# Both orders of real and imaginary part from TensorE's transposes in a fused retention, state-space and FFN block

## The reference

```python
h = rmsnorm(x, norm_mix_g)
proj = h @ w_in                      # 2048 -> 5120: q, k, v, g, u of 1024 each
y_ret = retention_group(rope(q), rope(k), v, g, ret_gn_g)
y_ssm = s5_group(u, ...)             # 64 groups of 16 channels, 64 complex states each
x = x + concat([y_ret, y_ssm]) @ w_out
h = rmsnorm(x, norm_ffn_g)
x = x + (silu(h @ w_gate) * (h @ w_up)) @ w_down     # 2048 -> 5632 -> 2048
return rmsnorm(x, norm_final_g)
```

## Time and profile before

| | |
|---|---|
| median of 3 runs | 1171.8 us (1170.96 to 1172.73) |
| the profiled execution | 1172.48 us, of which the span of its records is 1170.7 us |
| PE busy | 1139.4 us, 97% of the span, 5632 matmuls |
| PE weight loads busy | 933.6 us, 80% |
| DVE busy | 714.3 us, 61% |
| ACT busy | 528.9 us, 45% |
| POOL busy | 91.8 us, 8% |
| mean granted TensorE clock | 0.987 |
| DMA | 226.37 MB, mean 193 GB/s |

### The profile page before, as it was taken

One profiled execution on the slowest core, in us unless ns is written; L12 is line 12 of the kernel. 1 busy time (PEld: TensorE's weight loads), 2 busy tenths in 40 slices (PEclk: granted clock), 3 DMA queues, 4 the chain that ended last, 5 costly groups with the idle time before them and its releaser, 6 DMA issues.

```text
span 1170.7 us, 15157 instructions
## 1 busy us (share of the span) xinstructions
PE 1139.4 (97%) x5632; PEld 933.6 (80%) x5632; DVE 714.3 (61%) x776; ACT 528.9 (45%) x617; POOL 91.8 (8%) x132
## 2 busy tenths in 40 slices
PE   8999969999999999999999999999999999999996
PEld 6777747788988888888888888888888888888885
DVE  7998787744774664555564645555464645555465
ACT  6756424344663554433434343443434343343443
POOL 8120231330100000000000000000000000000001
PEclk9998988999999999999999999999999999999998
DMA  9783676676565567656566666656566666656652
GB/s 360 263 228 105 195 203 197 192 212 197 186 206 179 184 180 219 195 181 196 181 195 183 193 183 193 196 181 196 180 195 181 193 184 193 188 187 190 187 186 90
DMA packets 115416, 226.37 MB, mean 193 GB/s; under 512 B 8625, under 2 KB 13105, under 8 KB 114737
## 3 DMA queue, kind: packets, MB, share of 16 engines
q1 hardware_dynamic: 110816, 214.80, 59.6%
q0 software_dynamic: 4128, 10.36, 3.4%
q10 hardware_dynamic: 432, 0.67, 0.2%
HBM read 218.59 MB, written 5.11 MB: 191 GB/s over the span
## 4 chain that ended last, share of the span: by engine, by line
PE 89%; DVE 4%; DMA 3%; issue 1%; ACT 1%; POOL 0%; SPq 0%; POOLq 0%; ACTq 0%
PE ps L1329 28%; PE ps L1331 27%; PE ps L1330 27%; DMA raw<-in_w_in 2%; DVE w_lo L743 1%; DMA swapped<-state 1%; PE ps L1551 1%; PE ps L1624 1%; PE ps L1626 1%; PE ps L1625 1%; PE ps L1466 1%; PE ps L1384 1%; PE ps L1449 1%; PE ps L1484 0%; PE ps L1424 0%
## 5 line engine op out<-in xcount | busy, mean ns | idle before, releaser
L743 DVE TENSOR_TENSOR w_lo<-raw,w_hi 128x1024 fp32r<-128x1024 f32 x384 | 468.3, 1224 | 412.0 <-ACT w_hi L412 411.7
L412 ACT ACTIVATE w_hi<-raw 128x1024 fp32r<-128x1024 f32 x384 | 407.0, 1060 | 593.7 <-PE ps L1331 549.3
L1329 PE MATMUL ps<-w_hi,actA_hi 128*128 128x512 f32 x576 | 229.9, 399 | 8.0 <-DVE w_lo L743 8.0
L1331 PE MATMUL ps<-w_hi,actA_lo 128*128 128x512 f32 x576 | 225.9, 392 | 0.0
L1330 PE MATMUL ps<-w_lo,actA_hi 128*128 128x512 f32 x576 | 225.5, 392 | 0.0
L1329 PE MATMUL ps<-w_hi,h2B_hi 128*128 128x512 f32 x352 | 139.0, 395 | 0.0
L1331 PE MATMUL ps<-w_hi,h2B_lo 128*128 128x512 f32 x352 | 138.8, 394 | 0.0
L1330 PE MATMUL ps<-w_lo,h2B_hi 128*128 128x512 f32 x352 | 138.8, 394 | 0.0
L1329 PEld LDWEIGHTS ps<-w_hi,actA_hi 128*128 128x128 f32 x576 | 109.0, 189 | 33.6 <-DVE w_lo L743 7.4
L1331 PEld LDWEIGHTS ps<-w_hi,actA_lo 128*128 128x128 f32 x576 | 108.8, 189 | 23.4
L1330 PEld LDWEIGHTS ps<-w_lo,actA_hi 128*128 128x128 f32 x576 | 109.0, 189 | 21.4
(11 more groups left out here) (239 smaller groups left out, 987.1 us busy)
## 6 DMA issues: line engine op xcount, KB each, us to landing
raw<-in_w_gate SPq DMA_DIRECT2D x88, 512.0 KB, 3.7
raw<-in_w_up SPq DMA_DIRECT2D x88, 512.0 KB, 3.7
raw<-in_w_down SPq DMA_DIRECT2D x88, 512.0 KB, 3.8
raw<-in_w_in SPq DMA_DIRECT2D x80, 512.0 KB, 4.9
raw<-in_w_out SPq DMA_DIRECT2D x32, 512.0 KB, 4.6
k_tab<-k_scratch POOLq DMA_DIRECT2D x64, 64.0 KB, 3.6
raw<-in_ssm_w_glu SPq DMA_DIRECT2D x8, 512.0 KB, 3.5
xT<-in_xT SPq DMA_DIRECT2D x8, 256.0 KB, 6.2
```

The lines of the kernel that those rows point to most:

```text
L412: nc.scalar.activation(w_hi[:, s % SPL], raw[:, s % RAW], ACT.Copy).then_inc(S["high_done"], 1)
L743: tt(w_lo[:, s % SPL], raw[:, s % RAW], w_hi[:, s % SPL].bitcast(F32), ALU.subtract).then_inc(S["low_done"], 1)
L1329: mm(o, x_hi, h, start=first, stop=False)
L1331: return mm(o, x_lo, h, start=False, stop=last)
```

## The change

- `inputs_back(b)` makes four transposes instead of two: of `vt` columns 0 to 127 and of columns 64 to 191. `vt` is 64 columns wider, and ACT fills it with two copies, the second one repeating the first 64 columns behind the rest. The results stand in bank 6 instead of half of bank 7, and ACT copies them to `state` and to `swapped`, so `v_free` counts two per batch.
- The first exchange by DMA goes; `scan_states(h)` waits for `v_free` 8 or 16 instead. The exchange between scan and turn-back stays. POOL also sets the first column of `swapped` to zero. The second exchange of POOL's queue comes right behind `load_k(0)`.
- The four ACT steps of a phase table are done in four chunks, one in each (26 to 29, 31 to 34).
- `cl` has a fourth slot in the room of `wbT`; `CL_SLOT` and `CL_PRIOR` say which table uses which slot, and which `y_batch` frees it. The decay loads, which share the room, wait for `y_mm` 3.
- K tables 0 and 1 go to banks 4 and 5. K0 waits for all of `wbT`, K2 and later ones for `v_free` 16.
- New places for turn steps, decays, scans, turn-back, `cl`, K, Y and the first two heads.

```diff
@@ -79,6 +79,8 @@
 CBUF, TBUF = 3, 2
+CL_SLOT = (0, 1, 3, 2, 0, 1, 2, 0)
+CL_PRIOR = (None, None, None, None, 0, 1, 3, 4)
 PARAM_AT = 9
...
@@ -86,21 +88,22 @@
 ANGLE_AT = (23, 27)
-TURN_AT = (26, 30)
-DECAYS_AT = (28, 38)
+TURN_AT = (26, 31)
+DECAYS_AT = (30, 36)
 FACTOR_AT = 29
-SCAN_AT = (33, 42)
-BACK_AT = (37, 45)
-CL_AT = (29, 31, 34, 44, 47, 50, 56, 60)
-K_AT = (31, 34, 37, 46, 49, 52, 58, 62)
-Y_AT = (42, 45, 47, 54, 57, 60, 66, 70)
-Y_BANK = (7, 7, 7, 7, 7, 7, 6, 6)
+SCAN_AT = (32, 40)
+BACK_AT = (35, 45)
+CL_AT = (30, 36, 38, 42, 47, 50, 55, 60)
+K_AT = (33, 38, 40, 44, 49, 52, 57, 62)
+Y_AT = (43, 47, 49, 53, 57, 65, 67, 71)
+K_BANK = (4, 5, 6, 6, 6, 6, 6, 6)
+Y_BANK = (7, 7, 7, 7, 7, 6, 6, 6)
 QK_AT = tuple(GRP * (gi + 1) + 3 for gi in (4, 5, 6, 7))
...
 DECAY_LOAD = (55, 55, 65, 66, 70, 71, 80, 81)
-HEAD_AT = (62, 63, 65, 66, 75, 76, 78, 79)
+HEAD_AT = (61, 62, 65, 66, 75, 76, 78, 79)
 STATS_AT = (67, 71, 81, 83)
...
@@ -203,9 +206,11 @@
             [("wbT", [P, 2, BG, P], F32)],
+            [("cl_extra", [P, BG, LOC + 1, CH], F32)],
             [("dec", [P, 2, TOK, SEQ], F32), ("sT", [P, 2, TOK, SEQ], F32)],
...
         wbT, dec, sT = (m[k] for k in ("wbT", "dec", "sT"))
+        cl_slots = [cl[:, i] for i in range(CBUF)] + [m["cl_extra"][:]]
         cl_t = sb("cl_t", [P, BG, LOC + 1, CH])
...
@@ -215,7 +220,7 @@
         dtmp = sb("dtmp", [P, GROUPS // 4, CH])
-        m = overlay([("rope", [P, TOK, 2, HEAD_DIM], F32)], [("vt", [P, 2, P], F32)])
+        m = overlay([("rope", [P, TOK, 2, HEAD_DIM], F32)], [("vt", [P, 2, P + STATE], F32)])
         rope, vt = m["rope"], m["vt"]
...
@@ -242,7 +247,6 @@
         d_b, d_c = sem("d_b"), sem("d_c")
-        d_swap = [sem(f"d_swap{i}") for i in range(2)]
         d_swap_back = [sem(f"d_swap_back{i}") for i in range(2)]
...
@@ -332,7 +336,7 @@
-                    sp.wait_ge(S["v_mm"], NB)
+                    sp.wait_ge(S["y_mm"], 3)
                 else:
...
@@ -432,20 +436,23 @@
-            def turn_tables(h):
-
-
-                act.wait_ge(S["angles_ready"], h + 1)
+            def turn_table(h, step):
+
+
                 c, s = flat(cos[h][:]), flat(sin[h][:])
-                nc.scalar.activation(s, c, ACT.Sin, scale=vec[:, V_TURN:V_TURN + 1]).then_inc(S["turn_step"], 1)
-                act.wait_ge(S["turn_step"], 4 * h + 1)
-                nc.scalar.activation(c, c, ACT.Sin, scale=3.1415925).then_inc(S["turn_step"], 1)
-                act.wait_ge(S["turn_step"], 4 * h + 2)
-                nc.scalar.activation(c, c, ACT.Square, scale=float(np.sqrt(2.0))).then_inc(S["turn_step"], 1)
-                act.wait_ge(S["turn_step"], 4 * h + 3)
-                if h == 0:
-                    act.wait_ge(S["const_ready"], 1)
-                nc.scalar.activation(c, c, ACT.Identity, bias=ones[:], scale=-1.0).then_inc(S["turn_step"], 1)
+                if step == 0:
+                    act.wait_ge(S["angles_ready"], h + 1)
+                    ins = nc.scalar.activation(s, c, ACT.Sin, scale=vec[:, V_TURN:V_TURN + 1])
+                else:
+                    act.wait_ge(S["turn_step"], 4 * h + step)
+                    if step == 1:
+                        ins = nc.scalar.activation(c, c, ACT.Sin, scale=3.1415925)
+                    elif step == 2:
+                        ins = nc.scalar.activation(c, c, ACT.Square, scale=float(np.sqrt(2.0)))
+                    else:
+                        act.wait_ge(S["const_ready"], 1)
+                        ins = nc.scalar.activation(c, c, ACT.Identity, bias=ones[:], scale=-1.0)
+                ins.then_inc(S["turn_step"], 1)
...
@@ -533,16 +540,18 @@
                             act.wait_ge(S["zero_ready"], 1)
-                        nc.scalar.activation(state[:, s5_group(b), 1:],
-                                             ps[:, 7, 2 * P:4 * P].rearrange("p (g k) -> p g k", g=BG)[:, :, 0:NCH - 1],
-                                             ACT.Copy).then_inc(S["v_free"], 1)
+                        for x, to in enumerate((state, swapped)):
+                            nc.scalar.activation(to[:, s5_group(b), 1:],
+                                                 ps[:, 6, 2 * P * x:2 * P * (x + 1)].rearrange("p (g k) -> p g k", g=BG)
+                                                 [:, :, 0:NCH - 1], ACT.Copy).then_inc(S["v_free"], 1)
                     if n == V_AT[b] + 4:
...
                             act.wait_ge(S["vT_mm"], b)
-                        nc.scalar.activation(vt[:], ps[:, 7, 0:2 * P].rearrange("p (a s) -> p a s", a=2), ACT.Copy
-                                             ).then_inc(S["vt_ready"], 1)
+                        sums = ps[:, 7, 0:2 * P].rearrange("p (a s) -> p a s", a=2)
+                        nc.scalar.activation(vt[:, :, 0:P], sums, ACT.Copy).then_inc(S["vt_ready"], 1)
+                        nc.scalar.activation(vt[:, :, P:], sums[:, :, 0:STATE], ACT.Copy).then_inc(S["vt_ready"], 1)
                     if n == K_AT[b] + 4:
...
@@ -551,7 +560,7 @@
                             act.wait_ge(d_kst[b % 2], 16 * (b // 2))
-                        nc.scalar.activation(kst_w[:, b % 2, :, LOC - 1:], ps[:, 6, 0:2 * P]
+                        nc.scalar.activation(kst_w[:, b % 2, :, LOC - 1:], ps[:, K_BANK[b], 0:2 * P]
                                              .rearrange("p (h d c) -> p h d c", h=2, c=CH), ACT.Copy
...
@@ -564,8 +573,8 @@
                 for h in range(2):
-                    if n == TURN_AT[h]:
-                        turn_tables(h)
+                    if 0 <= n - TURN_AT[h] < 4:
+                        turn_table(h, n - TURN_AT[h])
                     if n == DECAYS_AT[h]:
...
@@ -901,7 +910,7 @@
-                dve.wait_ge(d_swap[h], 32)
+                dve.wait_ge(S["v_free"], NB * (h + 1))
                 dve.wait_ge(S["turn_step"], 4 * h + 4)
...
@@ -927,16 +936,18 @@
-                o = cl[:, b % CBUF]
+                o = cl_slots[CL_SLOT[b]]
                 if b == 0:
...
                     dve.wait_ge(S["cl_ready"], b)
-                if b == 2:
+                if CL_SLOT[b] == 2:
                     dve.wait_ge(S["wb_mm"], NB)
-                if b >= CBUF:
-                    dve.wait_ge(S["y_mm"], b - CBUF + 1)
+                if CL_SLOT[b] == 3:
+                    dve.wait_ge(S["v_mm"], NB)
+                if CL_PRIOR[b] is not None:
+                    dve.wait_ge(S["y_mm"], CL_PRIOR[b] + 1)
                 tt(o, of_groups(c_tab[:, 0], b, LOC + 1), of_powers(pr, b, 0, LOC + 1), ALU.mult)
...
@@ -1234,7 +1245,8 @@
             pool.wait_ge(S["pe_done"], 1)
-            nc.gpsimd.memset(state[:, :, 0], 0.0).then_inc(S["zero_ready"], 1)
+            nc.gpsimd.memset(state[:, :, 0], 0.0)
+            nc.gpsimd.memset(swapped[:, :, 0], 0.0).then_inc(S["zero_ready"], 1)
...
@@ -1249,12 +1261,12 @@
-            def swap(h, signal):
+            def swap(h):
...
                     pool.dma_start(y[STATE * a:STATE * (a + 1)], x[STATE * (1 - a):STATE * (2 - a)]
-                                   ).then_inc(signal[h], 16)
+                                   ).then_inc(d_swap_back[h], 16)
...
@@ -1276,18 +1288,14 @@
                 u_local(h)
-            pool.wait_ge(S["v_free"], HB)
-            swap(0, d_swap)
             pool.wait_ge(S["scanned"], 1)
-            swap(0, d_swap_back)
+            swap(0)
             store_k(0)
             load_k(0)
+            pool.wait_ge(S["scanned"], 2)
+            swap(1)
             store_k(1)
-            pool.wait_ge(S["v_free"], NB)
-            swap(1, d_swap)
             load_k(1)
-            pool.wait_ge(S["scanned"], 2)
-            swap(1, d_swap_back)
             for b in range(2, 6):
...
@@ -1391,22 +1399,29 @@
                     pe.wait_ge(S["b_pad_ready"], 1)
+                    pe.wait_ge(S["wbT_ready"], NB)
                 else:
                     pe.wait_ge(S["kpsum_free"], b)
+                if K_BANK[b] == 6:
+                    pe.wait_ge(S["v_free"], 2 * NB)
                 for g in range(BG):
...
                     gg = BG * b + g
-                    ins = mm(ps[32 * q:32 * q + 32, 6, P * h:P * (h + 1)],
+                    ins = mm(ps[32 * q:32 * q + 32, K_BANK[b], P * h:P * (h + 1)],
                              b_re[:, gg:gg + 2].rearrange("p a c -> p (a c)"),
-                             cl[:, b % CBUF, g, 0:LOC].rearrange("p d c -> p (d c)"), start=True, stop=True)
+                             cl_slots[CL_SLOT[b]][:, g, 0:LOC].rearrange("p d c -> p (d c)"), start=True, stop=True)
                 ins.then_inc(S["k_mm"], 1)
...
-                pe.wait_ge(S["vt_ready"], b + 1)
-                for a in range(2):
-                    ins = tr(ps[:, 7, P * (2 + a):P * (3 + a)], vt[:, a], ident[:])
+                pe.wait_ge(S["vt_ready"], 2 * b + 2)
+                if b:
+                    pe.wait_ge(S["v_free"], 2 * b)
+                for x in range(2):
+                    for a in range(2):
```

(10 more changed lines are left out.)

## The result

The changed kernel takes 1157.4 us (median of 4 runs, 1156.22 to 1158.89) against 1172.1 us before (median of 4 runs, the profiled one among them): ratio 0.9876, 95% interval 0.9859 to 0.9893, so 14.7 us less. The profiled execution took 1156.22 us with a span of 1154.4, against 1172.48 and 1170.7: 16.3 us less. It is the fastest of the four.

What follows compares the result with a forecast made beforehand. PE was taken as the bound, with 15.3 us of idle plus slow clock, behind ACT's turn steps and the serial chain to the second scan. Sum: 1172.48 − 17.2 + 1.2 + 0.8 = 1157.3; range 1151 to 1163.

Steps and rivals of the forecast that it cites:

- Turn steps spread: Chunk 25: one ACT step instead of four ahead of high(27); PE idles 0.7 us instead of 3.43, clock stays.
- PE up to the last inputs: PE's work up to inputs_back(7), which begins at 133.5 and ends at 133.9, against 139.35 before.
- Load 41 and copies: From the end of the last transposes to the second scan at chunk 40: 7.6 us, so it starts at 141.5.
- DVE early at the scan: Ahead of the second scan DVE is ready at about 137.7 and idles 3.8 us.
- Who waits between chunk 40 and 41: K2's wait in chunk 40 is 0.4 us, hidden; PE's longest wait is w_lo at chunk 41, 2 to 3 us.
- Chunk 47: Chunk 47 starts at 169.5 instead of 186.69, 17.2 us earlier.
- Y moved: The second y_batch now stands in chunk 47, before done by then: a debt of 1.2 us.
- Clock: Behind the 2.3 us idle at chunk 41 the clock may fall, costing 0 to 1.6 us; 0.8 taken.
- Rival 1: Load 41 and its copies come before DVE is free, no wait replaces the old ones: 1153.2, chance 0.17.
- Rival 2: New waits at chunks 25, 33, 41 each run 1 us over, clock low 10 us: 1162.5, chance 0.16.
- Rival 3: DVE is the bound all through and the exchange was covered: 1171, chance 0.03.
- Rival 4: Slower: three new idles keep PE at 1.2 GHz from chunk 33 to 47: 1197, chance 0.04.

Runs made afterwards that it cites:

- the moved wait: Changed kernel with SP's wait for the last inputs_back and the rope load ahead of load 43 instead of load 41: 1151.9 us, ratio 0.9837.
- K2 moved: Changed kernel with K2 in chunk 41 instead of 40: 1158.0 us, ratio 0.9890.
- old places: Changed kernel with scans and first turn-back at chunks 33, 42 and 37 instead of 32, 40 and 35: 1158.1 us, ratio 0.9890.
- second half by DMA: Changed kernel with the old DMA exchange put back as a wait ahead of the second scan alone: 1163.8 us, ratio 0.9941.
- steps in one piece: Changed kernel with the four ACT steps of each phase table again in one piece, at chunks 26 and 31: 1162.2 us, ratio 0.9919.
- both exchanges by DMA: Changed kernel's schedule, but both exchanges ahead of the scans by DMA as before, two transposes per batch: 1169.4 us, ratio 0.9985.
- one exchange by DMA: Two kernels: changed kernel with the old DMA exchange back ahead of one scan alone; first scan 1163.3 us, second scan 1163.8 us.
- transposes twice: Changed kernel with every group of four transposes of vt made twice, 64 instead of 32: 1159.3 us, ratio 0.9898.
- phase steps alone: Kernel before with only the four ACT steps of each phase table spread over four chunks: 1168.5 us against 1171.7, ratio 0.9978.

## Why the prediction was right

Forecast 1157.3, measured 1157.4. That the two are 0.1 apart is luck. The sum starts from the profiled execution of the kernel before, so it stands against the profiled execution of the changed one: it forecast 15.2 us less, and 16.3 were measured. Of its terms, chunk 47 was 0.7 too early, the debt 0.7 too high and the clock 0.8 too high; the two first cancel, and 0.3 lies in no term. What was right is the mechanism and the size of its main term, 17.2 us forecast up to chunk 47 and 16.5 measured. Step by step:

- **Turn steps spread: right.** Idle ahead of the transposes of chunk 25: forecast 0.7, measured 0.43. ACT's copies are done at 87.4, forecast 87.5. The clock stayed.
- **K0's new wait: right.** Forecast 1.0, measured 0.92, behind `wbT`.
- **PE up to the last inputs: right.** Forecast 133.5 to 133.9, measured 133.2 to 133.7.
- **Load 41 and copies: mis-sized by 0.6.** Forecast 7.6 us from the transposes to the scan. Measured 141.86 − 133.68 = 8.2: the load took 6.13 instead of 5.31. Why is open. Rope and three more loads left close by in both kernels, but POOL's eight loads of K tables had all left ahead of load 41 before, and six of them leave behind it now; before, a store of POOL left 0.5 us behind it (POOL's queue before, then after; load 41 leaves at 139.77 and 134.08):

```profile
136.07 4.20 POOL L1273 DMA_DIRECT2D k_tab<-k_scratch  x8 [4.01 <-DMA k_scratch<-kst]
```

```profile
133.21 4.21 POOL L1285 DMA_DIRECT2D k_tab<-k_scratch  x8 [2.26 <-DMA k_scratch<-kst]
```

The prediction did not look at what POOL's queue would send at that time. No run moved these loads away.

- **DVE early at the scan: right.** Forecast 137.7, idle 3.8; measured 137.24, idle 4.62. The back step's wait was put at 2 to 4 and took 1.85; `v_free` 8 at 1, took 1.16.
- **Who waits between chunk 40 and 41: the place was wrong, the end was right.** PE's longest wait was forecast as `w_lo` at chunk 41, 2 to 3 us; it was the one ahead of K2. K2's wait was sized at 0.4 and took 1.80: load 42 went out 1.3 us behind load 41 and landed later still, and ACT makes the copy of K1 behind it. The clock fell behind *that* idle, not behind one at chunk 41, where only 0.17 was left of the 2.3. Both cover the same wait for DVE, which moving K2 showed: 4.20 us in one piece, the same `w_lo`, and no gain.
- **Chunk 47: right within 0.7.** Forecast 169.5, measured 170.21. The scan was 0.4 late, PE having been 0.2 early and the load and copies 0.6 longer; the rest came between the scan and chunk 47.
- **Y moved: over-sized.** The debt was put at 1.2. Measured: PE's lead over before was 16.5 us at chunk 47 and 16.0 from chunk 68 on, a debt of 0.5. The second `y_batch` was compared with an empty chunk 47, but there before had its third one; it fell due at chunk 49 with 0.9, and K6 and Y4 in one chunk gave some back.
- **Clock: over-sized, within its range.** I took 0.8 of a range of 0 to 1.6. It was at half for 3.41 us and cost nothing, for DVE's `w_lo` was later still (0.17 us of idle at chunk 41). One reading under this term was not right: in the kernel before, the second slow stretch began at 171.77, behind the idle of 2.05 alone, and not behind the pair 2.05 and 4.13. That makes a fall behind 2.3 us more likely than the range between 0.69 and 3.43 let it look.
- **Rival 1 (1153.2) was the moved wait**, not the change: its mechanism, load 41 before DVE is free, came true when the load was sent earlier, with 1151.9. That is below its 1153.2 and above the 1151 that it named with the slow clock near 162 us. The trace of the kernel before does have such a stretch, at 1.2 GHz from 161.53 to 164.94, behind the 5.00 us of idle. **Rival 2** (new waits each 1 us over) came true at K2 alone, which was not among the places it named. **Rival 3** (the exchange was covered) is refuted by the 12 us for putting it back. **Rival 4** (clock stuck) had half clock for 3.41 us, where it needed 24.

What stays open: the median gain is 14.7, that of the two profiled executions 16.3. The runs of one kernel differ by up to 4 us, and each kernel has one trace. Those traces name one thing that varies: load 41 took 6.13, 6.08 and 6.15 us in three kernels (changed, K2 moved, old places), and 8.02 and 9.13 in two others with nearly the same loads around it (second half by DMA, steps in one piece). In the last, PE was 5.7 us late at chunk 38 and 8.7 at chunk 41, by the 3.0 us that the load took longer. Why it varies is not shown.

## What to carry to other kernels

When an exchange stands ahead of a step on an in-order engine, price everything from the last input of the exchange to the first output behind that step, and look for whichever load or copy now ends that chain: here an unrelated wait for rope on the load queue was worth 4.4 to 5.5 us more with one line changed. Look at all queues there: what another engine sends at the same time was not in this forecast. An idle stretch of PE is only worth its length if the engine that it waits for next would be earlier too; taking away K2's 1.8 us gained nothing. Side work in one piece ahead of an eviction should be cut into steps, one for each chunk; that was worth 3.2 us by itself here, and 4.7 within the change.

## What the runs showed of the hardware

**Clock.** Idles on PE that brought a stretch at 1.2 GHz with them were dearer than their length: two of 5.75 and 7.44 us cost 5.0 us more in slow work. The granted clock fell behind idles of, among others, 1.80 us (changed kernel), 2.05 (the kernel before, at 171.77), 2.00 (both exchanges by DMA), 2.14 and 3.08 (one exchange by DMA), 3.60 (old places) and 4.20 (K2 moved). It stayed at 2.4 GHz behind 1.65 and 1.05 (transposes twice), 1.30 (old places), and 1.27 and 1.14 (phase steps alone). What PE did between its idles differs among these kernels, so they give no limit that would hold elsewhere.

**Transposes.** Transposes of 128x128 in a row cost 0.105 us each, though each record lasts 0.272.

**Loads.** A load of 512 KB alone on its queue took 3.53 us from issue to landing (load 40 of the changed kernel). Load 41 took 6.13 with a load of 256 KB just ahead of it, three more of 512 KB behind it and POOL's small loads around it, and from 5.45 (transposes twice) to 9.13 (steps in one piece) over the kernels that kept its wait.
